# Where the SBUF buffers of a two-block transformer kernel begin: small tables first, large buffers at multiples of 2,048 bytes

## The reference

```python
# first block, per layer                      (modulation vectors from cond @ ada_w)
h = rms_norm(x, g) * (1 + sc1) + sh1
x = x + g1 * hybrid_mixer(h, ...)             # gated linear attention + retention, w_in and w_out
h = rms_norm(x, g) * (1 + sc2) + sh2
y = swiglu(h, ffn_w1, ffn_w3, ffn_w2)         # layer 0: width 2,816
y = moe_swiglu(h, router_w, moe_w1, ...)      # layer 1: 8 experts of width 1,408, top 2
x = x + g2 * y
# second block, per layer, with 256 more context tokens beside the 256
h_x = h_x + 0.5 * mx[2] * ffn1(pre(h_x, ...)) # width 2,816
ox = short_conv_mixer(nx, ...)                # layer 0
ox = latent_attention(q_x, k_all, v_all) @ mla_w_o   # layer 1
h_x = h_x + 0.5 * mx[8] * ffn2(pre(h_x, ...))
```

## Time and profile before

| | |
|---|---|
| median of 3 runs | 2835.23 us |
| lowest to highest | 2834.12 to 2836.9 us |
| the profiled execution | 2839.29 us |
| its span, first to last instruction | 2837.6 us |
| mean granted clock of PE | 0.989 |

### The profile page before, as it was taken

The page is one execution under the profiler, slowest core; times in us unless marked ns, Lnnn a source line. Parts: engine busy times, 40 slices in busy tenths (PEclk is TensorE's granted clock), DMA queues, the critical chain, the costliest instruction groups (busy, mean ns, idle before and its releaser), DMA issues.

```text
span 2837.6 us, 43022 instructions
## 1 busy us (share of the span) xinstructions
PE 2720.8 (96%) x17542; PEld 2445.7 (86%) x17542; DVE 1913.8 (67%) x2703; ACT 1182.6 (42%) x1510; POOL 118.1 (4%) x227
## 2 busy tenths in 40 slices
PE   3979999999999999899999999999999999999999
PEld 3879998899999999888888888888888888886999
DVE  5877778765777788777477445764666646675655
ACT  3436445453443477642132424422334222255543
POOL 0010000000000000000000000000000000000000
PEclk9989999999999999999999999999999999999999
DMA  7676766635676698745355223453534534311554
GB/s 296 220 244 228 263 228 213 232 135 169 235 239 209 230 347 309 259 145 187 132 184 169 83 93 103 153 170 122 166 136 137 169 122 159 120 60 46 176 186 144
DMA packets 116619, 511.97 MB, mean 180 GB/s; under 512 B 12608, under 2 KB 16064, under 8 KB 116304
## 3 DMA queue, kind: packets, MB, share of 16 engines
q1 hardware_dynamic: 81776, 381.92, 39.5%
q0 software_dynamic: 32112, 117.45, 12.5%
q10 hardware_dynamic: 2544, 9.96, 0.9%
HBM read 508.24 MB, written 1.05 MB: 179 GB/s over the span
## 4 chain that ended last, share of the span: by engine, by line
PE 78%; DVE 11%; ACT 4%; issue 3%; DMA 2%; ACTq 0%; DVEq 0%; POOLq 0%
PE PS L2099 22%; PE PS L2101 22%; PE PS L2100 22%; DVE wlo L1102 5%; ACT whi L575 2%; PE PS L2293 1%; DMA ada_first<-in_adastream 1%; PE PS L2290 1%; PE PS L2289 1%; DVE ada L1134 1%; PE PS L2194 1%; DMA ada<-in_adastream 1%; PE PS L2195 1%; PE PS L2198 1%; DVE PS L1134 1%
## 5 line engine op out<-in xcount | busy, mean ns | idle before, releaser
L575 ACT ACTIVATE whi<-raw 128x1408 fp32r<-128x1408 f32 (+2 forms) x540 | 718.1, 1342 | 778.9 <-PE PS L2101 719.3
L1102 DVE TENSOR_TENSOR wlo<-raw,whi 128x1408 fp32r<-128x1408 f32 (+2 forms) x540 | 839.8, 1577 | 217.0 <-ACT whi L575 216.1
L2099 PE MATMUL PS<-h_hi,whi 128*128 128x256 f32 (+1 forms) x2656 | 859.2, 324 | 15.5 <-DVE wlo L1102 8.4
L2100 PE MATMUL PS<-h_lo,whi 128*128 128x256 f32 (+1 forms) x2656 | 858.7, 323 | 0.0
L2101 PE MATMUL PS<-h_hi,wlo 128*128 128x256 f32 (+1 forms) x2656 | 858.6, 323 | 0.0
L2099 PEld LDWEIGHTS PS<-h_hi,whi 128*128 128x128 f32 x2656 | 499.6, 188 | 64.0 <-DVE wlo L1102 11.4
L2100 PEld LDWEIGHTS PS<-h_lo,whi 128*128 128x128 f32 x2656 | 499.6, 188 | 43.1 <-issue 0.2
L2101 PEld LDWEIGHTS PS<-h_hi,wlo 128*128 128x128 f32 x2656 | 500.1, 188 | 39.6
L2099 PE MATMUL PS<-hid_hi,whi 128*128 128x256 f32 (+1 forms) x1298 | 415.3, 320 | 4.3 <-DVE wlo L1102 4.3
L2100 PE MATMUL PS<-hid_lo,whi 128*128 128x256 f32 (+1 forms) x1298 | 414.6, 319 | 0.0
L2101 PE MATMUL PS<-hid_hi,wlo 128*128 128x256 f32 (+1 forms) x1298 | 414.4, 319 | 0.0
(11 more groups left out here) (464 smaller groups left out, 3245.8 us busy)
## 6 DMA issues: line engine op xcount, KB each, us to landing
raw<-in_wstream SPq DMA_DIRECT2D x243, 704.0 KB, 4.5
raw<-in_wstream SPq DMA_DIRECT2D x176, 768.0 KB, 5.6
ada<-in_adastream POOLq DMA_DIRECT2D x222, 512.0 KB, 4.5
raw<-in_wstream SPq DMA_DIRECT2D x121, 512.0 KB, 4.0
ada_first<-in_adastream ACTq DMA_DIRECT2D x6, 1536.0 KB, 22.9
X<-in_xT SPq DMA_DIRECT2D x1, 1024.0 KB, 13.9
X<-in_ctxT SPq DMA_DIRECT2D x1, 1024.0 KB, 5.6
cond<-in_c_rows POOLq DMA_DIRECT2D x1, 1024.0 KB, 5.7
```

Source lines behind the costliest of these rows:

```text
L575: nc.scalar.activation(whi[:, (q + dp) % SLOTS, 0:n], raw[:, (q + dp) % RAW_SLOTS, 0:n], ACT.Copy).then_inc(hi_split, 1)
L1102: nc.vector.tensor_tensor(wlo[:, (q + dp) % SLOTS, 0:n], raw[:, (q + dp) % RAW_SLOTS, 0:n], whi[:, (q + dp) % SLOTS, 0:n].bitcast(F32), AL ...
L2099: mm(o, left[0], right[0], start=start, stop=False)
L2100: mm(o, left[0], right[1], start=False, stop=False)
```

## The change

The order of the `sb` calls is changed. The small tables (`tables`, `mod1`, `mod2`, `amp1`, `amp2`, `gate2`, `ms`, `root`, `rstd`, with what overlays them) move from the middle of the partition to its front. A `pad` of 64 bytes follows, so that `raw` begins at byte 12,288. `wroute_lo` moves from the end of the mixer's range to overlay one of the tables, and `gt`, `gi`, `rt` and `order` stand behind `turned_hi`, `turned_lo` and `picks` and no longer ahead of them. No instruction is added, removed or moved: every engine's list is the same, with the same waits, and only addresses in operands differ.

```diff
+        tables = sb("tables", [PART, VECS + CONSTS])
+        vec, con = tables[:, 0:VECS], tables[:, VECS:VECS + CONSTS]
+        mod1 = sb("mod1", [PART, 2, 48])
+        with ExitStack() as s:
+            wga = sb("wga", [PART, 2, KD, RANK], F32, s)
+        mod2 = sb("mod2", [PART, 2, 72, 2])
+        amp1 = sb("amp1", [PART, 2, 2, KD])
+        with ExitStack() as s:
+            wroute_lo = sb("wroute_lo", [PART, KD, N_EXPERTS], F32R, s)
+        amp2 = sb("amp2", [PART, 2, 3, KD, 2])
...
+        rstd = sb("rstd", [PART, 32])
+        sb("pad", [PART, 16])
         raw = sb("raw", [PART, RAW_SLOTS, SLOT * PART])
         whi = sb("whi", [PART, SLOTS, SLOT * PART], F32R)
         wlo = sb("wlo", [PART, SLOTS, SLOT * PART], F32R)
...
         stage_b = sb("stage_b", [PART, 2, BOTH])
-        tables = sb("tables", [PART, VECS + CONSTS])
...
-        rstd = sb("rstd", [PART, 32])
...
                 gated = sb("gated", [PART, 2, SEQ], F32, s2)
+                turned_hi = sb("turned_hi", [PART, 2, D], F32R, s2)
+                turned_lo = sb("turned_lo", [PART, 2, D], F32R, s2)
+                picks = sb("picks", [PART, 2, SPARSE, PART], F32R, s2)
                 gt = sb("gt", [PART, 2, 64], F32, s2)
...
-                turned_hi = sb("turned_hi", [PART, 2, D], F32R, s2)
-                turned_lo = sb("turned_lo", [PART, 2, D], F32R, s2)
-                picks = sb("picks", [PART, 2, SPARSE, PART], F32R, s2)
...
-                wroute_lo = sb("wroute_lo", [PART, KD, N_EXPERTS], F32R, s2)
```

More of the change, by code:

```diff
@@ L194, in sem @@
             return ctx.enter_context(nc.semaphore(name))
+        tables = sb("tables", [PART, VECS + CONSTS])
[8 more added lines that the diff above has]
+        amp2 = sb("amp2", [PART, 2, 3, KD, 2])
+        with ExitStack() as s:
+            wroute = sb("wroute", [PART, KD, N_EXPERTS], F32, s)
+        gate2 = sb("gate2", [PART, 2, 3, KD, 2])
+        ms = sb("ms", [PART, 36])
+        root = sb("root", [PART, 32])
+        rstd = sb("rstd", [PART, 32])
+        sb("pad", [PART, 16])
         raw = sb("raw", [PART, RAW_SLOTS, SLOT * PART])
```

## The result

The changed kernel takes 2847.61 us (median of 8 runs, 2845.12 to 2850.45), the kernel before on the same chips 2836.64 (8 runs, 2832.7 to 2840.1). The ratio is 1.0039, with a 95% interval of 1.0028 to 1.005: 11 us or 0.4% slower, clear of noise. The profiled execution of the kernel after takes 2847.39 us, its span is 2845.7.

A forecast was written before the change was run, and what follows sets the result against it. PE was taken to set the pace, with 78% of the last chain. Terms -10.4 + 16.6 + 5.3 - 1.0 = +10.5 us, put against the median of 2835.23, gave 2845.7 us; range 2805 to 2857.

The forecast's parts named there:

- item 1: 4746 matmuls of 512 columns, nearly all in 1215 to 2510 us: distance 64 to 0, 228.9 to 226.7 ns, -10.4 us.
- item 2: 256-column matmuls across the stages, distance 64 to 0: 117.8 to 120.0 ns each, +16.6 us in sum.
- The three quarters for the experts: 600 to 970 us: +6.7 us of slower 256-column matmuls counted as +5.0, about a quarter of the chain being DVE's.
- item 3: 1584 matmuls of 256 columns in 970 to 1215 us, distance 192 to 0: 113.3 to 120.0 ns, half of +10.6 taken, +5.3.
- item 4: Panels and `ada` rows written from multiples of 256 bytes; mainly `ada_first` at the start: -1.0 us, between +1 and -11.
- the prediction's estimate of 2: By the skill's rule, `ada_first` rows of 4,096 bytes take 16 transactions for 17: 2 us for the whole transfer.
- item 5: DVE and ACT: splits read and write as before since `raw`, `whi`, `wlo` keep their distances, the rest is short: 0 us.
- Distance 0 is the fast place: Rival: at distance 0, 256 columns lock at 113.3 ns and 512 at 226.7; 2791 us, chance 0.13.
- Places don't matter: Rival: PE's paces stay, their differences being accidents of stalls, and only the DMA gain is left; 2834 us, chance 0.16.
- Only the 512-column part comes: Rival: 256-column paces stay at 117.8 and 113.3 ns, leaving -10.4 and -1.0 us; 2824 us, chance 0.12.
- a distance of 0 that behaves otherwise at 0 than at 128: What the forecast couldn't carry: all its rows at distance 0 begin at 128 mod 256; no size given.

The follow-up runs named there:

- e1: Changed kernel with a 64-byte gap ahead of the activations, distance to weights back to 64 mod 256: 2835.28 us, 0.9996 of the kernel before.
- e3: Changed kernel with a 192-byte gap ahead of the activations (activations less weights 192 mod 256): 2848.31 us, 1.0041 of the kernel before.
- e8: Changed kernel with 256-token stages' tensors at distance 192, `few` at 64, 512-column tensors and `y` at 0: 2820.63 us, 0.9941 of the kernel before.
- e2: Changed kernel with everything from `raw` on moved by 64 bytes, distances kept at 0: 2849.96 us, 1.0041 of the kernel before.
- e9: Changed kernel with `whi` and activations at 192 mod 256 and `wlo` at 0: 2853.26 us, one run, against 2836.36 before.
- e5: Changed kernel with a 32-byte gap ahead of the activations: 2859.71 us, one run, against 2837.0 for the kernel before.
- e7: Changed kernel with a 64-byte gap ahead of the 256-token stages' tensors alone, 512-column tensors at distance 0: 2828.5 us, 0.9967 of the kernel before.
- e4: Changed kernel with a 128-byte gap ahead of the activations, putting `y` against `whi` at 0: 2864.19 us, 1.009 of the kernel before.

## Why the prediction was right

**The time.** 2845.7 us forecast, 2847.61 measured; a loss of 10.5 us forecast, 11.0 by the medians, and 8.1 by the two profiled spans (2845.7 less 2837.6). The mechanism was right, but agreement to half a microsecond is luck. The six stages for which the prediction had a pace lost 14.4 us (11.7 against the second profile of the kernel before) where its shares sum to 11.0, and the start, priced at -0.5 in all, and attention, which does not repeat, gave 5.9 of them back.

**What bounds the kernel.** The prediction went by start-to-start steps and not by the durations that the page gives. In the earlier trace rows a matmul of 256 columns has a duration of 0.28 us, and it has 0.28 in the kernel after too, while the step went from 117.8 to 120.0 ns: the duration is modelled and the step is what time is made of. Reading places beside steps turned three small samples into a price for 15,000 matmuls.

**512 columns** (item 1, -10.4 us on the path). The step was right to 0.1 ns (226.67), with luck: the 8 steps of the earlier trace rows are the last of 31 such steps without a wait in that stage, and the mean of all 31 is 229.9. The stretch as a whole took 5.7 us less than in the first profile and 7.2 less than in the second; forecast with its 256-column part -7.3. That part holds 1211 products of `h` or `hid` with weights and not 1407. The prediction gave no price to the value projections, 192 matmuls of 512 columns with the weights moving; they went from distance 192 to 0 and from 233.3 to 227.6 ns, about -1 us in the two mixers.

**256 columns, distance 64 to 0** (item 2, +16.6). The step was right, 120.00. First layer +3.0 for +3.2, last stage +3.7 for +3.8, dense experts +6.0 (+4.7 against the second profile) for +5.0, second mixer +0.4 or -0.5 for +1.0; 847 of its 1258 matmuls are these passes, about 100 us of the 180 and not a third, but the value projections and the waits give that back. The three quarters for the experts, taken from DVE's part of the chain, were near enough.

**Weights moving** (item 3, +5.3, bounds +2 and +10.6). +7.0 and +8.1 in the stage: half was too little, two thirds to three quarters of it reached the path. The waits for DVE in this stage hide less than the 14.8 us of idle time seemed to promise.

**DMA** (item 4, -1.0). The start of the kernel gained more, 3.3 us up to matmul 1278, with +0.5 of slower PE in it. In the chain of the kernel after:

```profile
8.63 36.64 DMA ada_first<-in_adastream
```

36.64 us for the 38.07 of the earlier trace rows; the second profile of the kernel before has 38.12. Over all kernels, the last of the six transfers into `ada_first` takes 36.3 to 37.1 us in each of the eight in which `raw`, `ada` and `X` begin at a multiple of 256 (after, e1, e3 to e8) and 37.8 to 38.1 in each of the four profiles in which they begin 64, 128 or 192 off (e2, e9, before, twice). The place of `ada_first` itself does not order them: it stood at 0, 64, 192, 128, 32, 96, 0 and 0 in the first group. The Trainium skill ("DMA: Bandwidth & Descriptors", "How a descriptor splits into AXI transactions") lets the first transaction of a piece that starts off a multiple of 256 bytes begin at the multiple below it. A gain of some 1.3 us in 38 agrees with the prediction's estimate of 2 in sign, but it should have followed `ada_first`'s own place, and the section speaks of bytes that are fetched, while only the place of writing changed. So the rule does not explain which kernels gain, and the cause stays open.

This gain is not the start's 3.3 us. Matmul 60, at about 60 us, starts 1.1 us earlier than before, about what the transfer gained. But 2.2 us more come at about 190 us, in one wait of PE for DVE, which is shorter in the kernel after than in any other (6.2 to 7.5 us). The views of PE's waits from 177 to 250 us, before and after (us in all, times, longest):

```profile
PE PS L2375 <- DVE mix L1547: 6.5, 1, 6.5
PE PS L2377 <- DVE mix L1549: 4.3, 1, 4.3
```

And in e5, e7 and e8, which have the short transfer too, the chain does not run through it: matmul 60 starts between 0.3 us earlier and 0.6 later than before, and the first stage takes 249.2 to 250.9 us for 250.0. In the other five it starts 1.1 to 1.8 us earlier. So the forecast of 1 us for the transfer was of the right size, and the rest of the start's gain is not explained. In e1_gap64, which keeps the short transfer and has the old paces, the whole kernel is at 0.9996 of before: within what can be measured.

**DVE and ACT** (item 5, 0). The splits of the most common panel, first in the kernel before, then in the kernel after; the means of one, 1620 and 1378 ns, are the same:

```profile
L1102 DVE TENSOR_TENSOR wlo<-raw,whi 128x1408 fp32r<-128x1408 f32 x247 | 394.9, 1620 | 124.4 <-ACT whi L575 124.4
L575 ACT ACTIVATE whi<-raw 128x1408 fp32r<-128x1408 f32 x249 | 341.7, 1378 | 592.1 <-PE PS L2101 540.2 <-PE PS L2293 50.7
L1104 DVE TENSOR_TENSOR wlo<-raw,whi 128x1408 fp32r<-128x1408 f32 x247 | 394.8, 1620 | 123.8 <-ACT whi L577 123.8
L577 ACT ACTIVATE whi<-raw 128x1408 fp32r<-128x1408 f32 x249 | 341.7, 1378 | 591.1 <-PE PS L2103 539.2 <-PE PS L2295 51.3
```

Busy time of DVE is 1914.0 us for 1913.8, of ACT 1182.5 for 1182.6.

**The rivals.** *Distance 0 is the fast place* was wrong: at 256 columns no run at distance 0 settled at 113.3 in any kernel here; 120.0 is the pace of all of them. *Places don't matter* was wrong by e1 and e2 together, and by `h` and `y` in e4. The Trainium skill ("SBUF — State Buffer", "Who interferes with whom") calls PE's two read ports independent and says that PE never waits on anyone, which gives no reason for any such difference; yet at 512 columns PE's means without any semaphore wait range from 226.7 to 234.2 ns with the distance of its own two operands. Whether one read waits for the other inside the chip is not shown. *Only the 512-column part comes* was wrong for this kernel, but it is what e7_mix64 was made to do. What the prediction feared, a distance of 0 that behaves otherwise at 0 than at 128, did not come: after (0), e2 (64) and the earlier trace rows (128) agree on 120.0.

## What to carry to other kernels

Where matmuls ran back to back here, the step from start to start depended on where moving and stationary operands begin relative to each other, modulo 256 bytes: in the means by up to 3% at 512 columns and 5% at 256. Round addresses are not the goal: in this kernel they made the 512-column matmuls 1% faster and the 256-column ones 2% slower. Look for steps in the timeline of the kernel at hand, sort them by distance and by columns, and give each stage its own gap; it costs a line of allocation and gave 0.6% here, and 0.3% with one gap of 64 bytes.

## What the runs showed of the hardware

- The step of a 128 x 128 matmul in float32r without waits: at 512 columns 226.7 ns at distance 0, 228.9 at 64, 232.8 to 234.2 at the other distances tried. At 256 columns 113.3 to 120.05.
- At 256 columns and distances 64 and 192 there are two steady paces, 113.3 and 117.8 ns. The same code on the same addresses ran at either, for 100 matmuls and more. Of 206 runs of 45 or more steps all under 125 ns (`h` or `hid` moving; before, e1, e3, e8) all but 2 keep one pace once they have settled, so the pace is taken at a restart; what in a restart decides is not shown. At distance 0 there is one, 120.0.
- Good and bad distances are not the same for 256 and 512 columns: 192 is the best for one and among the worst for the other, 0 the other way round; 96 is bad for both.
- A shift finer than 64 bytes matters: at distance 32 the 512-column step is 233.3 ns, with 226.8 at 0 and 228.9 at 64. Whether through the distance or through the operand's own place is not shown.
